# Half of the root multiplications at both sides of the last mixer move from VectorE to GpSimd

## The reference, cut to what matters

```python
def sublayer(h_res, j, fn, res_w):
    h = rms_norm_2(h_res, norm_g[l, 2 * j]) * (1.0 + scale) + shift
    y = rms_norm_2(fn(h), norm_g[l, 2 * j + 1])
    return h_res + res_w * gate * y
...
x = sublayer(x, 0, lambda h: swiglu(h, ...), 0.5)
x = sublayer(x, 1, mixer, 1.0)
x = sublayer(x, 2, lambda h: swiglu(h, ...), 0.5)
```

## Time and profile before

| | |
|---|---|
| median of 3 runs | 2402.71 us (2402.67 to 2404.18) |
| time of the profiled execution | 2402.43 us |
| its span, first to last instruction | 2400.6 us |
| TensorE, VectorE, ScalarE busy | 98%, 60%, 43% of the span |
| GpSimd busy | 0.2 us |

### The profile page before, as it was taken

One profiled execution on the slowest core, in us unless ns is written; L12 is line 12 of the kernel. 1 busy time (PEld: TensorE's weight loads), 2 busy tenths in 40 slices (PEclk: granted clock), 3 DMA queues, 4 the chain that ended last, 5 costly groups with the idle time before them and its releaser, 6 DMA issues.

```text
span 2400.6 us, 30910 instructions
## 1 busy us (share of the span) xinstructions
PE 2343.3 (98%) x11342; PEld 1982.9 (83%) x11342; DVE 1439.0 (60%) x2073; ACT 1037.9 (43%) x1562; POOL 0.2 (0%) x4
## 2 busy tenths in 40 slices
PE   7899999999999999999999999999999998999999
PEld 5788888888888886888888878888877676888887
DVE  7777777757566677867566564333356985433333
ACT  5655555544233246854223233322347565332333
POOL 0000000000000000000000000000000000000000
PEclk9999999999999999999999999999999999999999
DMA  4222222225355532024444523332322112223231
GB/s 154 73 80 79 78 78 79 81 87 179 127 166 166 166 117 77 1 71 167 156 151 157 176 84 105 106 102 93 113 71 71 53 53 71 85 100 114 88 114 71
DMA packets 71246, 249.57 MB, mean 104 GB/s; under 512 B 9824, under 2 KB 10336, under 8 KB 70752
## 3 DMA queue, kind: packets, MB, share of 16 engines
q1 hardware_dynamic: 68912, 247.28, 30.7%
q10 hardware_dynamic: 2224, 0.79, 0.1%
HBM read 245.94 MB, written 2.10 MB: 103 GB/s over the span
## 4 chain that ended last, share of the span: by engine, by line
PE 89%; DVE 6%; ACT 3%; issue 1%; DMA 0%; ACTq 0%; SPq 0%; DVEq 0%
PE psum L438 26%; PE psum L439 26%; PE psum L440 26%; PE psum L502 2%; DVE w_lo L1700 1%; PE psum L856 1%; PE psum L555 1%; PE psum L533 1%; PE psum L562 1%; PE psum L910 1%; DVE nrm L1677 1%; PE psum L960 0%; DVE x L2214 0%; PE psum L940 0%; ACT w_hi L1040 0%
## 5 line engine op out<-in xcount | busy, mean ns | idle before, releaser
L438 PE MATMUL psum<-h_hi,w_hi 128*128 128x512 f32 x1768 | 683.8, 387 | 8.6 <-DVE w_lo L1700 4.5
L439 PE MATMUL psum<-h_lo,w_hi 128*128 128x512 f32 x1768 | 670.6, 379 | 0.0
L440 PE MATMUL psum<-h_hi,w_lo 128*128 128x512 f32 x1768 | 670.6, 379 | 0.0
L1040 ACT ACTIVATE w_hi<-raw 128x1024 fp32r<-128x1024 f32 x385 | 403.0, 1052 | 463.8 <-PE psum L440 454.7
L1700 DVE TENSOR_TENSOR w_lo<-raw,w_hi 128x1024 fp32r<-128x1024 f32 x385 | 466.0, 1220 | 136.8 <-ACT w_hi L1040 135.3
L438 PEld LDWEIGHTS psum<-h_hi,w_hi 128*128 128x128 f32 x1768 | 334.6, 189 | 68.3 <-issue 9.6
L439 PEld LDWEIGHTS psum<-h_lo,w_hi 128*128 128x128 f32 x1768 | 334.8, 189 | 47.3 <-issue 2.6
L440 PEld LDWEIGHTS psum<-h_hi,w_lo 128*128 128x128 f32 x1768 | 334.5, 189 | 47.6
L2192 DVE TENSOR_TENSOR s_s<-s_g,psum 128x512 f32<-128x512 f32 x44 | 30.2, 687 | 281.9 <-issue 223.8
L438 PE MATMUL psum<-f_hi,w_hi 128*128 128x512 f32 x512 | 194.0, 379 | 0.0
L439 PE MATMUL psum<-f_lo,w_hi 128*128 128x512 f32 x512 | 194.0, 379 | 0.0
(11 more groups left out here) (340 smaller groups left out, 3253.1 us busy)
## 6 DMA issues: line engine op xcount, KB each, us to landing
raw<-stream SPq DMA_DIRECT2D x385, 512.0 KB, 3.5
ada_raw<-ada_in SPq DMA_DIRECT2D x72, 512.0 KB, 4.1
x<-x_in SPq DMA_DIRECT2D x2, 1024.0 KB, 6.3
out<-x SPq DMA_DIRECT2D x8, 256.0 KB, 2.4
a_mask<-mask_in SPq DMA_DIRECT2D x1, 1024.0 KB, 9.3
crow<-crow_in SPq DMA_DIRECT2D x2, 512.0 KB, 5.1
gatew<-gate_in ACTq DMA_DIRECT2D x2, 256.0 KB, 3.8
a_cos<-rope_in SPq DMA_DIRECT2D x1, 256.0 KB, 7.7
```

The lines of the kernel that those rows point to most:

```text
L438: nc.tensor.matmul(o, whi, xh, start=start, stop=False)
L439: nc.tensor.matmul(o, whi, xl, start=False, stop=False)
L440: return nc.tensor.matmul(o, wlo, xh, start=False, stop=stop)
L1040: A(w_hi[:, slot(u0), :], raw[:, slot(u0), :], ACT.Copy).then_inc(S["hi"], 1)
```

## The change

Of the eight tiles at each of the two sites, GpSimd multiplies tiles 1, 3, 5 and 7 by the root. VectorE multiplies tiles 0, 2, 4 and 6 and makes all eight additions, in the old order of tiles. GpSimd starts when the root is there and goes through its four tiles without waiting for VectorE; before each it waits for `Y_g`, ScalarE's signal that the tile has got its constants. VectorE waits for `G_y` before it adds an odd tile. The last sublayer's end stays on VectorE.

```diff
         def y_added(yy, k, step=1):
 
-            return after("Y_x", 2 * (KT * yy + k) + step)
+            return after("Y_x", 12 * yy + 3 * (k // 2) + (step if k % 2 == 0 else 2))
...
-            return after("Y_x", 4 * KT + (k if k < LAST_ON_PE else LAST_ON_PE + 2 * (k - LAST_ON_PE)))
+            return after("Y_x", 24 + (k if k < LAST_ON_PE else LAST_ON_PE + 2 * (k - LAST_ON_PE)))
...
         @block.gpsimd
         def _(pool):
             credits(pool, "lo")
+            for yy in range(2):
+                pool.wait_ge(*after("Y_rst", yy))
+                for k in range(1, KT, 2):
+                    pool.wait_ge(*after("Y_g", 4 * yy + k // 2))
+                    nc.gpsimd.tensor_tensor(y[:, k, :], y[:, k, :], rst[:, 1, :], ALU.mult).then_inc(S["G_y"], 1)
...
-                A(y[:, k, :], y[:, k, :], ACT.Copy, scale=ada_col(yy, 2, k))
+                last = A(y[:, k, :], y[:, k, :], ACT.Copy, scale=ada_col(yy, 2, k))
+                if yy < 2 and k % 2:
+                    last.then_inc(S["Y_g"], 1)
...
                 dve.wait_ge(*after("Y_rst", yy))
                 for k in range(KT):
-                    V.tensor_tensor(y[:, k, :], y[:, k, :], rst[:, 1, :], ALU.mult).then_inc(S["Y_x"], 1)
-                    dve.wait_ge(*y_added(yy, k, 0))
+                    if k % 2 == 0:
+                        V.tensor_tensor(y[:, k, :], y[:, k, :], rst[:, 1, :], ALU.mult).then_inc(S["Y_x"], 1)
+                        dve.wait_ge(*y_added(yy, k, 0))
+                    else:
+                        dve.wait_ge(*after("G_y", 4 * yy + k // 2))
                     V.tensor_tensor(x[:, k, :], x[:, k, :], y[:, k, :], ALU.add).then_inc(S["Y_x"], 1)
```

More of the change, by code:

```diff
@@ L253, in build @@
         for n in ("F_r F_s F_hi F_lo F_x Sw_g Sw_s Sw_hi Sw_lo Sw_out Sw_y R_x MO_y N_sq N_ms N_ln N_rst N_s N_hi N_lo "
-                  "F_t N_ac Y_ac Y_sq Y_ms Y_ln Y_rst Y_x").split():
+                  "F_t N_ac Y_g G_y Y_ac Y_sq Y_ms Y_ln Y_rst Y_x").split():
             S[n] = ctx.enter_context(nc.semaphore(n))
@@ L340, in y_added @@
         def y_added(yy, k, step=1):
-            return after("Y_x", 2 * (KT * yy + k) + step)
+            return after("Y_x", 12 * yy + 3 * (k // 2) + (step if k % 2 == 0 else 2))
         LAST_ON_PE = 5
         def last_scaled(k):
-            return after("Y_x", 4 * KT + (k if k < LAST_ON_PE else LAST_ON_PE + 2 * (k - LAST_ON_PE)))
+            return after("Y_x", 24 + (k if k < LAST_ON_PE else LAST_ON_PE + 2 * (k - LAST_ON_PE)))
         def last_added(k):
-            return after("Y_sq", 3 * KT + k) if k < LAST_ON_PE else after("Y_x", 4 * KT + LAST_ON_PE + 2 * (k - LAST_ON_PE) + 1)
+            return after("Y_sq", 3 * KT + k) if k < LAST_ON_PE else after("Y_x", 24 + LAST_ON_PE + 2 * (k - LAST_ON_PE) + 1)
         def last_bank(k):
```

## The result

The changed kernel is slower: 2409.20 us (median of 14 runs, 2407.59 to 2410.61) against 2403.42 us for the kernel before (14 runs beside them, 2402.27 to 2406.08). The ratio is 1.0023, with a 95% interval of 1.0015 to 1.0031. That is +5.8 us, where +4.5 us and 2407.2 us had been predicted. The profiled execution shown here took 2410.18 us, 7.8 more than the one of before.

The account below looks back on a forecast made before the run. VectorE's chain from the root on was taken to bound both sites; four GpSimd turns of 1.22 us less 2.63 us removed work, twice, gave +4.5 us and 2407.2 us, range 2397.0 to 2411.0.

Parts of the forecast that it names:

- the turns: At both sites GpSimd multiplications and VectorE instructions exclude each other at SBUF: +4.5 us in all; chance 0.31.
- rival 1: Turns at SBUF costing over 1.26 us each, so slower by more than 0.2% (4.8 us); chance 0.29.
- The signs named in advance: VectorE records beside GpSimd's stretched from 0.69 to about 1.9 us or late, four a site, then the old pace.
- The removed work: VectorE loses four multiplications a site, 2.88 us, of which 0.25 goes back in TensorE's last sums: 2.63 saved.
- The price of a GpSimd multiplication: Each 128 x 512 multiplication on GpSimd estimated at 1.22 us, bounds 0.685 and 1.76; four a site.
- Every multiplication appears in the chain with its whole length: Each GpSimd multiplication adds its full 1.22 us to a site's chain: 4.88 - 2.63 = 2.25 us a site.
- Rival 1's reason: Every handover between VectorE and GpSimd adds a start, 0.15 us a turn, giving 5.7 us and 2408.4 us.
- this stayed inside a pair's slack: ScalarE's waits for the sum two tiles back delay odd squares by 0.1 to 0.2 us, costing nothing.
- The clock, a small fourth case: Long turns leave TensorE without sums at the sites; a fallen clock or slow first GpSimd instruction: chance 0.04.
- The hint from the shorter one-input instructions: VectorE takes 0.487 us with one SBUF input, 0.685 to 0.692 with two, so seems to use both ways in.
- rival 3: Turns by the column: only streaming parts exclude each other, about +0.3 us a site, 2403.3 us, no change; chance 0.16.
- rival 2: GpSimd and VectorE run side by side undisturbed at the sites: -5.3 us, 2397.4 us; chance 0.20.

Follow-up runs that it names:

- one_tile: Changed kernel, but GpSimd multiplies only tile 7 at each site; 2406.36 us in one run.
- keep_clock: Changed kernel plus 24 unused matmuls at each site to keep TensorE busy; 2406.62 us, ratio 1.0013 to the kernel before.
- psum_turns: Changed kernel with VectorE taking even tiles first and reading the root and its own products from PSUM; 2400.04 us, ratio 0.9986 to the kernel before.
- pool_one_input: Changed kernel, but GpSimd multiplies the odd tiles by 0.5, reading one input, in place of the root; 2403.60 us in one run.
- psum_three: As psum_turns, but GpSimd takes only tiles 1, 3 and 5, added between the others; 2399.43 us, ratio 0.9984 to the kernel before.
- pool_fill: Changed kernel, but GpSimd fills the odd tiles with zeros, reading nothing, in place of multiplying; 2399.28 us, ratio 0.9983 to the kernel before.
- even_first: Changed kernel with the tile order of psum_turns, but root and products read from SBUF; 2410.29 us, ratio 1.0029 to the kernel before.

## Why the prediction was right, step by step

**The direction and the mechanism held, and the time lies in the range; that it came as near as 2 us is in part luck.** Three terms were off, and not all the same way: the turns cost 1.7 us less than the sum had (8 x 0.21), a fallen clock that had no term cost 2.75, and the ends of the sites 0.4. The forecast was the turns; rival 1, the same mechanism above 0.2%, is what the median shows, though the interval reaches down to 0.15%. The signs named in advance came: four records a site are stretched, to 1.64 to 1.75 us in place of the 1.9 foreseen, and the old pace follows.

**The removed work, 2.63 us a site.** Right: the fill, in which nothing contends, took 2.68 us off the window.

**The price of a GpSimd multiplication, 1.22 us.** Right as a price alone, 1.22 us by its starts. That it fits to the hundredth is luck: the figure was borrowed from VectorE's pace over 1024 columns, and no run shows that GpSimd reads its two inputs one after the other. The estimate worked out from the Trainium skill, page GPSIMD Engine Reference, section 3.1 Elementwise, was 1.11; the measured distance is 0.11 above it.

**Every multiplication appears in the chain with its whole length.** This step of the forecast was mis-sized. Four turns cost (11.83 - 7.80) = 4.03 us in VectorE's part, 1.01 each in place of 1.22: a part of a turn passes beside the other engine's work, about 0.13 us at each handover by the records of one_tile, and only the rest excludes VectorE. Rival 1's reason, a handover on top of each turn, is refuted by that. Without anything else a site would have cost 4.03 - 2.63 = +1.4 us, the kernel +2.8. The windows of keep_clock, at full clock, have +1.6 a site: the missing 0.2 is the end of the site, where ScalarE and TensorE take turns at two buffers. The prediction had thought that this stayed inside a pair's slack.

**The clock, a small fourth case.** Here the prediction was wrong in weight: it gave 0.04 to a fallen clock and a slow start together, and its sum has no term for the clock. Its reading of the earlier trace rows was also too strong, as a 9 there stands for 90% or more; for the sites themselves does show 1.00. The clock fell at both sites, in the sums themselves, and was back at 1.00 before the next sublayer's products began. It costs 1.25 and 1.5 us. With it the windows add up: 2 x (1.4 + 0.2) + 1.25 + 1.5 = 5.95 us, against 5.97 in the two sites and 5.8 by the medians.

**Turns of what kind.** The hint from the shorter one-input instructions led to the right case, but was no evidence for it: with one input in SBUF and one in PSUM the same two-input instructions take 0.69 us as well (psum_turns), so their length doesn't tell which way the inputs come in. What decides it are the runs: VectorE's records with two SBUF inputs are stretched by 1.0 us beside a GpSimd multiplication and not at all beside a fill, and those with one SBUF input not at all (0.69 us). The rule cited from the Trainium skill, page SBUF — State Buffer, section Who interferes with whom, agrees with this in who disturbs whom. That the other engine is blocked for the whole instruction doesn't quite fit: 1.01 of 1.22 us excluded VectorE here, and beside GpSimd's one-input instructions of 1.69 us VectorE's records grew by only 0.3 to 0.4. Sharing by the column (rival 3) had put VectorE's part at 10.7 us; it was 11.83, between that and the 12.7 of whole turns at 1.22, so the sum alone doesn't rule it out. The records do: the multiplication that ran when GpSimd began kept 0.69 us, and the record behind it took the whole delay. Side by side (rival 2) needs the inputs moved, as in psum_turns.

## What to carry to other kernels

Before work moves from VectorE to GpSimd, list what VectorE will execute meanwhile and where its inputs lie: GpSimd, the slower engine, blocked the faster one here for nearly its own length, 1.01 of 1.22 us. If VectorE's second input can be in PSUM, such a split can be a gain: -4.0 us with three tiles here, against +5.8. And where a chain of small operations feeds TensorE, price the pauses between its matmuls as well as the chain: the lost clock level cost as much here (2.75 us) as the turns less the work they removed (2.8 us).

## What the runs showed that was not expected

- One pause of 1.68 us in TensorE's work was followed by a lower granted clock (0.86 over the site, in one_tile). With pauses of 1.68, 0.55 and 1.27 us it was 0.50 from 1785.1 to 1791.5, the level of 1.2 GHz. With pauses of 1.02, 0.33, 0.49 and 0.36 us (pool_one_input) it stayed at 1.00, and filling the pauses with 24 short matmuls kept it there too.
- Late in the mixer, from 1980 to 1995, where TensorE is busy 10.9 to 12.3 of 15 us, the clock was 1.00 in the profiled executions of before and of the changed kernel, 0.89 in keep_clock, psum_turns and psum_three, and 0.77 to 0.85 in pool_fill, pool_one_input, one_tile and even_first, though the kernels don't differ there. From the first site's last sum to the second site's first multiplication it took 234.3 to 234.6 us in the first five and 236.9 to 237.0 in the last four. Why is open, but 2.6 us is as much as some of the effects measured here, so a single run tells little unless its sites are read apart.
- A GpSimd instruction with one input took 1.69 us on average beside VectorE, hardly less than one with two (1.71), though it cost VectorE less than half as much (0.46 us against 1.01).
